# Neighbourhood bias read from the table by sixteen shifted transfers instead of band matmuls

## What is computed

```python
r0 = jnp.clip(r - kh // 2, 0, rows - kh)                 # rows = kh = 4, so r0 = 0
c0 = jnp.clip(c - NA_WIN_W // 2, 0, GRID_W - NA_WIN_W)   # 16 columns
col_ok = (c[None, :] >= c0[:, None]) & (c[None, :] < c0[:, None] + NA_WIN_W)
s = jnp.einsum('bhrqd,bhrikd->bhrqik', qg, kg) * (d ** -0.5)
dr = key_rows - r[:, None] + (NA_WIN_H - 1)
dc = jnp.clip(c[None, :] - c[:, None], -(NA_WIN_W - 1), NA_WIN_W - 1) + (NA_WIN_W - 1)
bias = rpb[:, dr[:, None, :, None], dc[None, :, None, :]]
s = jnp.where(col_ok, s + bias, -jnp.inf)
```

## Time and profile before

| | us |
|---|---|
| plain runs, median of 3 | 3781.74 |
| lowest and highest | 3781.71 and 3783.3 |
| profiled execution, its span | 3784.1 |
| TensorE matmuls busy in it | 3541.0 (94%) |
| VectorE busy | 2168.7 (57%) |
| ScalarE busy | 1618.5 (43%) |
| POOL busy | 419.4 (11%) |
| DMA engines busy, by weight queue | 50.6% |

### The profile page before, as it was taken

How to read it: one execution, slowest core, us unless ns; L and a number is a source line. 1 busy time by engine, 2 the same in 40 slices (tenths; PEclk the granted TensorE clock), 3 DMA queues, 4 the chain that set the end, 5 groups by cost and what they waited for, 6 DMA issues and landing times.

```text
span 3784.1 us, 45287 instructions
## 1 busy us (share of the span) xinstructions
PE 3541.0 (94%) x16538; PEld 2940.2 (78%) x16538; DVE 2168.7 (57%) x2397; ACT 1618.5 (43%) x1953; POOL 419.4 (11%) x330
## 2 busy tenths in 40 slices
PE   7899989999999888989899999999999978999979
PEld 6677778887888766777788888888888777788767
DVE  4976564555555587665555545565447544645544
ACT  3444334343434335433444443444445433355543
POOL 0614000000000060140100000000000041000100
PEclk9999999999999999999999999999989889999989
DMA  6444456655565555445566666556646200565534
GB/s 224 137 150 148 163 173 186 195 185 182 185 188 184 165 151 149 134 150 187 203 190 188 192 186 192 185 187 193 194 136 175 87 6 31 165 193 169 160 104 134
DMA packets 310641, 615.57 MB, mean 163 GB/s; under 512 B 19082, under 2 KB 19113, under 8 KB 308539
## 3 DMA queue, kind: packets, MB, share of 16 engines
q1 hardware_dynamic: 306144, 591.73, 50.6%
q0 software_dynamic: 4320, 21.34, 1.8%
HBM read 610.90 MB, written 2.10 MB: 162 GB/s over the span
## 4 chain that ended last, share of the span: by engine, by line
PE 81%; DVE 13%; ACT 4%; issue 2%; DMA 0%; POOL 0%; SPq 0%; DVEq 0%; ACTq 0%
PE ps_unit L252 24%; PE ps_unit L254 24%; PE ps_unit L253 24%; DVE sb_w_lo L236 4%; DVE sb_conv_y L901 2%; PE ps_mix L2324 2%; ACT sb_w_hi L229 2%; PE ps_mix L975 1%; PE ps_mix L376 1%; PE ps_mix L530 1%; DVE sb_h_s L1167 1%; PE ps_mix L1995 1%; PE ps_mix L2322 0%; DMA sb_raw<-in_w_in_dram 0%; PE ps_mix L2679 0%
## 5 line engine op out<-in xcount | busy, mean ns | idle before, releaser
L236 DVE TENSOR_TENSOR sb_w_lo<-sb_raw,sb_w_hi 128x1024 fp32r<-128x1024 f32 x1120 | 1407.7, 1264 | 1311.6 <-ACT sb_w_hi L229 1305.9
L229 ACT ACTIVATE sb_w_hi<-sb_raw 128x1024 fp32r<-128x1024 f32 x1120 | 1183.1, 1060 | 1838.1 <-PE ps_unit L254 1823.6
L252 PE MATMUL ps_unit<-sb_w_hi,sb_a_hi 128*128 128x512 f32 x3456 | 1383.1, 400 | 87.1 <-DVE sb_w_lo L236 56.0
L253 PE MATMUL ps_unit<-sb_w_lo,sb_a_hi 128*128 128x512 f32 x3456 | 1361.4, 394 | 0.0
L254 PE MATMUL ps_unit<-sb_w_hi,sb_a_lo 128*128 128x512 f32 x3456 | 1361.1, 394 | 0.0
L252 PEld LDWEIGHTS ps_unit<-sb_w_hi,sb_a_hi 128*128 128x128 f32 x3456 | 660.1, 191 | 242.9 <-DVE sb_w_lo L236 49.5
L254 PEld LDWEIGHTS ps_unit<-sb_w_hi,sb_a_lo 128*128 128x128 f32 x3456 | 658.5, 191 | 141.3
L253 PEld LDWEIGHTS ps_unit<-sb_w_lo,sb_a_hi 128*128 128x128 f32 x3456 | 660.0, 191 | 132.8
L252 PE MATMUL ps_unit<-sb_w_hi,sb_f_hi 128*128 128x512 f32 x1024 | 399.9, 391 | 0.0
L254 PE MATMUL ps_unit<-sb_w_hi,sb_f_lo 128*128 128x512 f32 x1024 | 398.6, 389 | 0.0
L253 PE MATMUL ps_unit<-sb_w_lo,sb_f_hi 128*128 128x512 f32 x1024 | 398.4, 389 | 0.0
(11 more groups left out here) (455 smaller groups left out, 2142.7 us busy)
## 6 DMA issues: line engine op xcount, KB each, us to landing
sb_raw<-in_w_ff_dram SPq DMA_DIRECT2D x512, 512.0 KB, 3.8
sb_raw<-in_w_in_dram SPq DMA_DIRECT2D x224, 512.0 KB, 3.8
sb_raw<-in_e_w_in_dram SPq DMA_DIRECT2D x112, 512.0 KB, 3.6
sb_raw<-in_o_w_in_dram SPq DMA_DIRECT2D x112, 512.0 KB, 3.7
sb_raw<-in_w_out_dram SPq DMA_DIRECT2D x64, 512.0 KB, 4.4
sb_raw<-in_e_w_out_dram SPq DMA_DIRECT2D x32, 512.0 KB, 4.4
sb_raw<-in_o_w_out_dram SPq DMA_DIRECT2D x32, 512.0 KB, 4.7
sb_raw<-in_e_w_mem_kv_dram SPq DMA_DIRECT2D x16, 512.0 KB, 4.5
```

What stands on the lines that cost most here:

```text
L229: k.nc.scalar.activation(k.w_hi[:, slot], k.raw[:, j], ACT.Copy).then_inc(k.hi_ready, 1)
L236: k.nc.vector.tensor_tensor(k.w_lo[:, slot], k.raw[:, j], k.w_hi[:, slot].bitcast(F32), ALU.subtract).then_inc(k.lo_ready, 1)
L252: k.nc.tensor.matmul(acc, hi[:, kt, tokens], w_hi, start=kt == 0, stop=False)
L253: k.nc.tensor.matmul(acc, hi[:, kt, tokens], w_lo, start=False, stop=False)
```

## The change

The table's columns are reversed in the layout of the input. In the reversed table the bias of query column c is a run of 64 elements that starts c elements further on, so that partition c of a transfer reads 64 elements from an address one element above that of partition c - 1, for all 6 heads: 16 transfers (2 token tiles x 2 grid rows x 4 key rows) of 64 partitions x 6 heads x 64 elements write the whole of `na_bias`, with the key columns backward. A run reads past the row of the table into its neighbours; those elements lie outside the window. POOL issues the transfers in `pool_delta`, after waiting for `dn_scaled`. One add of the mask, also reversed, over the whole buffer takes the place of 24. The band constant, the transpose of the table with VectorE's copy of it, the 64 matmuls, their semaphores and two of the early transfers go. The score adds read the bias from its last column backward.

```diff
@@ even_maps
-    maps = [(k.na_t[:, h, :], k.na_t[:, HEADS + h, :], k.na_bias[:, h].rearrange("p t r c -> p t (r c)"),
+    maps = [(k.na_t[:, h, :], k.na_t[:, HEADS + h, :], from_last_column(k.na_bias[:, h]),
@@ pool_even_rows
-    for to, src in ((k.na_rows[:], d["na_rpb_2"][0].rearrange("h a b -> (h a) b")), (k.na_band[:], d["c_band"]),
-                    (k.na_window[:], d["c_window"]), (k.gain_rows[0:1, :], d["na_q_norm_2"]),
+    for to, src in ((k.na_window[:], d["c_window"]), (k.gain_rows[0:1, :], d["na_q_norm_2"]),
@@
+NA_BIAS = TT * 2 * GRID_ROWS * 16
+
+
+def pool_na_bias(pool, k):
+
+    rpb = k.dram["na_rpb_2"]
+    pool.wait_ge(*k.dn_scaled.next("pool"))
+    with k.nc.allow_non_contiguous_dma(reason="a window of the table for each query column"):
+        for t in range(TT):
+            for r in range(2):
+                for a in range(GRID_ROWS):
+                    row = WIN_H - 1 - (2 * t + r) + a
+                    src = bass.AP(rpb.tensor, rpb.offset + row * RPB_COLS + WIN_W - GRID,
+                                  [[1, GRID], [RPB_ROWS * RPB_COLS, HEADS], [1, GRID]])
+                    pool.dma_start(k.na_bias[r * GRID:(r + 1) * GRID, :, t, a, :], src).then_inc(*k.na_bias_in.up(16))
@@ pe_even_inputs
-    tensor.transpose(k.ps[0:RPB_COLS, 1, 0:HEADS * RPB_ROWS], k.na_rows[:],
-                     k.ident[0:HEADS * RPB_ROWS, 0:HEADS * RPB_ROWS]).then_inc(*k.na_tableT.up())
-    run(2)
-    pe.wait_ge(*k.na_table_kept.next("pe"))
...
-    for half in range(2):
-        if half:
-            run(5)
-            pe.wait_ge(*k.na_bias_kept.next("pe"))
-        for n in range(BIAS_ROUND):
...
-        last.then_inc(*k.na_toeplitz.up())
     run.rest()
-    pe.wait_ge(*k.na_bias_kept.next("pe"))
@@ dve_even_inputs
-    run(1)
-    dve.wait_ge(*k.dn_scaled.now())
-    for half in range(2):
-        run(1)
-        dve.wait_ge(*k.na_toeplitz.next("dve"))
...
+    run(59 - run.done)
+    dve.wait_ge(*k.na_bias_in.next("dve", NA_BIAS))
+    bias = k.na_bias[:].rearrange("p h t r c -> p (h t r) c")
+    v.tensor_tensor(bias, bias, k.na_window[:].unsqueeze(1).to_broadcast([P, HEADS * SEQ // P * GRID_ROWS, GRID]),
+                    ALU.add).then_inc(*k.na_bias_kept.up())
     run(max(61 - run.done, 0))
     dve_divide(dve, k, E_Q, 2 * HEADS + 2 * MEM_HEADS)
@@ dve_even_attention
     dve.wait_ge(*k.even_gated.next("dve"))
+    dve.wait_ge(*k.na_bias_kept.now())
@@ pool_delta
     g.memset(k.dn_u[:, :, SEQ + 2:DN_T], 0.0).then_inc(*k.dn_pad.up())
+    pool_na_bias(pool, k)
     pool.wait_ge(*k.dn_g_done.next("pool"))
@@ kernel
+    arrays["na_rpb_2"] = np.ascontiguousarray(arrays["na_rpb_2"][..., ::-1])
```

## The result

| | before | changed |
|---|---|---|
| plain runs of the first comparison, median | 3781.72 (4 runs) | 3749.55 (4 runs, 3748.72 to 3750.94) |
| ratio, 95% interval | | 0.9919, 0.9904 to 0.9933 |
| span of the profiled execution | 3784.1 | 3747.6 |
| VectorE's head scaling ends, after the delta heads' scaling | 70.0 | 42.7 |
| first score add starts, after the same | 80.0 | 52.6 |

The kernel became faster by 0.8%. The forecast was 3754.9 with a range of 3752 to 3769, so the measured time lies 5.4 us under the forecast and 2.5 under the low end. The two profiled spans differ by 36.5 us: 9.0 come before the end of the delta heads' scaling (2926.90 against 2917.94), 27.4 between it and the first score add, and 0.1 behind that. What lies in the 27.4 is shown first; the 9.0 are taken up with the experiments.

The account below looks back on a forecast made before the run. TensorE held 81% of the chain; in the changed stage VectorE's head scaling would end it, saving 26.8 us. Profiled span 3784.1 - 26.8 = 3757.3, less 2.4 for profiling, gives 3754.9 us, range 3752 to 3769.

Parts of the forecast that it names:

- the low end: Bottom of the forecast range, 3752: TensorE's 28.3 us saved in full plus a microsecond or two of clock at the transposes.
- The mechanism and its size: Even layer's input projection: without band matmuls and 24 bias adds, VectorE's head scaling ends the stage, 26.8 us sooner.
- TensorE's 28.3: Input projection: 13 blocks at 2.72 us take 35.4 instead of 63.7 once the band matmuls go.
- the low clock: Short band matmuls drop TensorE to 1.2 GHz until some 5 us after them; the change removes this.
- The add: One VectorE mask add of 128x3072 in place of 24 bias adds: 3.35 us, bounds 3.2 and 3.6.
- the backward reads: Six score adds reading the bias in steps of minus one element: taken as 0, at most 3.2 us.
- the early transfers: Two short transfers leave POOL's early list, bringing others forward 1.1 us; TensorE is busy there, so nothing gained.
- The transfers: Sixteen bias transfers from POOL at 0.9 us each, 14.4 in all, landing 13.6 us before needed; up to 1.75 each costs nothing.
- The fixed part: Rival: each transfer starts when the one before has landed, about 2.2 us each, 5.6 late, 3760.5; chance 0.05.
- The slow rivals: Transfers at 2.55, 3.0 to 3.8 or 5.1 us each: 3767.9 (chance 0.17), nothing gained (0.06), 3809 (0.08).
- the price I gave for no gain: Rival: transfers take 3.0 to 3.8 us each and the wait cancels TensorE's saving, within 7 us of 3781.7; chance 0.06.
- the last one: Final step: profiled 3757.3 less 2.4, the profiled execution's excess over the plain median, gives 3754.9.

Follow-up runs that it names:

- The last two runs: Changed kernel with each transfer's partitions reading six rows unshifted (3753.51), and with all six heads reading one row, shifted (3784.12); one run each.
- the two that bring the first score add 1.0 and 2.0 us forward: Changed kernel with GpSimd adding the mask instead of VectorE (3752.28), and with bias add after block 56, head scaling after block 59 (3754.67).

## Why the prediction was right, and where it was wrong

- **The mechanism and its size: right.** Forecast 26.8 us by VectorE's chain, measured 27.3 at the head scaling's end and 27.4 at the first score add. Counted from the delta heads' scaling: split ahead of the add done at 29.8 (forecast 30.1), add done at 33.1 (33.4), head scaling done at 42.7 (43.2). Of the first 0.3, 0.2 is ScalarE, whose rounding ahead of that split ends at 28.6 (forecast 28.8).
- **TensorE's 28.3, the low clock as part of it: right.** Its blocks end 39.8 after the delta heads' scaling, forecast 39.6, and the idle behind them is 2.97, forecast 3.6. That the clock fell because of the short matmuls is shown by the run that puts them back: it falls in the same two places (0.58 and 0.64).
- **The add, the backward reads, the early transfers: right.** 3.35, 0 and nothing.
- **The transfers: right in size, and for a reason that is shown in part.** The landing was forecast at 16.5 and came at 17.4, 0.96 a transfer instead of 0.9. That the spread of the reads over 3 KB keeps them fast was an argument from the nearest row. The last two runs show that reading six rows instead of one does it; half of those 3 KB, unshifted, is as fast.
- **The fixed part.** The Trainium skill, DMA: Bandwidth & Descriptors (Anatomy of one DMA), gives each transfer from POOL some 2.0 us. Here the soonest landed 2.7 us after its issue and the transfers came on at about 1 us each; the reading in which the fixed part is paid in a row is refuted.
- **The slow rivals: right on the price, wrong on the wait.** With one row the transfers take 3.5 to 3.7 us each, which is the price I gave for no gain, and the runs, one each, gave 3784 and 3786. But I let VectorE wait for the bias; in the run it was ScalarE, for weight loads queued on the same DMA engines.
- **The step that failed: the last one, from the profiled execution to the plain time, with the low end.** I took the profiled execution to be 2.4 over the typical run and put the low end at "TensorE's 28.3 in full and a microsecond or two of clock at the transposes". Both ask only the stage's terms how far the time could go down, and put the difference between executions at nothing. Three plain runs within 1.6 us of each other (3781.71 to 3783.3) hid it, though the prediction itself has 7.6 us as what a measurement tells from no change. The runs show more: 46 of the kernel before lie between 3772.79 and 3787.29, with a mean of 3780.2; ten of the changed kernel lie between 3747.02 and 3761.57, with a mean of 3752.2. The difference of the means, 28.0, is the stage's 27.4 within its own error (about 1.5, estimated from the spread of these runs). Against the mean of 3752.2 the forecast is 2.7 too high: 1.5 because the kernel before was placed at 3781.7, 0.6 in the stage, and 0.6 that is left over. The four runs of the first comparison lie another 2.6 under that mean; of the spread of single runs that is little, and no run tells chance from a difference between chips. A low end of 3745 would have taken the spread in (the low end of 3752, less the 7.4 by which the lowest of the 46 runs lies under their mean). Six of the ten runs are under 3752.

Open is what decides in which gaps of TensorE an execution meets the 1.2 GHz level. The traces show that it varies from one execution to the next in unchanged code, not why.

No variant beats the changed kernel by more than its runs differ: the two that bring the first score add 1.0 and 2.0 us forward gave 3752.28 and 3754.67.

## What to carry to other kernels

Short matmuls in the midst of a long row of full ones cost more than their own time, and an engine that ends just behind another takes its share of what is saved there: follow both up to the end of the stage. Before many partitions read a small table straight from memory, look from how many rows one transfer reads; where it was a single short one, every other load in flight paid for it. How close several rows may lie is not shown here. And ask how far executions of one kernel differ before giving a range: a few runs that agree don't tell it.

## What the runs showed of the hardware

- Many small reads of one place are slow, shifted start addresses or not: 3.5 to 3.7 us for 384 pieces of 256 bytes within 508 bytes, 0.96 with the same pieces on six rows 1860 bytes apart. While it lasts, the 512 KB weight loads of two tensors take 24.6 and 52.7 us (medians) to land, against 4.1 and 8.3.
- Beside a GpSimd add of 128x3072, one VectorE split of 128x1024 took 6.34 us instead of 1.23. GpSimd needs 6.87 for the add for which VectorE needs 3.35.
- The same unchanged stretch runs at clock 1.00 in one execution and at 0.89 in the next, and the split behind it moved by up to 9 us between executions of the two kernels, which have the same code there.
